# A two-block layer kernel: panel z behind panel k2, and the scan's exponential and norm moved in the written order

## The reference

```python
h = rmsnorm_2(x, norm_mix_w[l]) * (1 + sc_m) + sh_m
z, xbc, dt_raw, q, k, v = jnp.split(h @ w_in[l], IN_SPLITS_2, axis=-1)
y_ssd = ssd_mixer(z, xbc, dt_raw, ...)      # ends: rmsnorm_2(y * silu(z), norm_w)
y_att = chunk_attention(q, k, v, rel_bias[l])
x = x + g_m * (jnp.concatenate([y_ssd, y_att], axis=-1) @ w_out[l])
```

## Time and profile before

| | |
|---|---|
| median of 3 runs | 820.22 us (819.9 to 821.61) |
| the profiled execution | 820.22 us, span 818.5 us |
| TensorE busy | 797.6 us, 97% of the span |
| VectorE busy | 588.6 us, 72% |
| ScalarE busy | 496.8 us, 61% |
| GpSimd busy | 15.7 us, 2% |
| mean granted TensorE clock | 0.999 of full |
| HBM | 196 GB/s over the span |

### The profile page before, as it was taken

How to read it: one execution, slowest core, us unless ns; L and a number is a source line. 1 busy time by engine, 2 the same in 40 slices (tenths; PEclk the granted TensorE clock), 3 DMA queues, 4 the chain that set the end, 5 groups by cost and what they waited for, 6 DMA issues and landing times.

```text
span 818.5 us, 14145 instructions
## 1 busy us (share of the span) xinstructions
PE 797.6 (97%) x5904; PEld 742.7 (91%) x5904; DVE 588.6 (72%) x752; ACT 496.8 (61%) x745; POOL 15.7 (2%) x36
## 2 busy tenths in 40 slices
PE   8999999999999999999999999999999999999996
PEld 8988879999999879999998888899788999999885
DVE  5465776648766857887878896897776977787563
ACT  6778688558837456444344256856757776666452
POOL 3000000100200000000000000000000000000000
PEclk9999999999999999999999999999999999999999
DMA  8873534446452568889787992744251865646611
GB/s 277 303 230 133 191 119 154 156 154 218 165 185 104 160 199 266 270 294 300 254 299 277 340 355 94 238 153 152 98 164 53 281 191 170 193 145 205 226 57 52
DMA packets 105951, 161.13 MB, mean 197 GB/s; under 512 B 4496, under 2 KB 51872, under 8 KB 105888
## 3 DMA queue, kind: packets, MB, share of 16 engines
q1 hardware_dynamic: 105888, 160.24, 59.3%
HBM read 159.16 MB, written 1.06 MB: 196 GB/s over the span
## 4 chain that ended last, share of the span: by engine, by line
PE 85%; DVE 6%; ACT 5%; issue 2%; DMA 1%; SPq 0%; DVEq 0%; ACTq 0%
PE ps L1557 54%; PE ps L1560 22%; DVE wL L1031 2%; ACT wH L669 2%; PE ps L1491 2%; DVE arena L1031 2%; PE ps L1708 1%; ACT arena L916 1%; PE ps L1537 1%; DMA raw<-in_w_in 1%; PE ps L1675 1%; DVE arena L1034 1%; PE ps L1755 1%; PE ps L1752 1%; DVE res L1031 1%
## 5 line engine op out<-in xcount | busy, mean ns | idle before, releaser
L1031 DVE TENSOR_TENSOR wL<-raw,wH 128x2048 fp32r<-128x2048 f32 (+2 forms) x133 | 282.9, 2131 | 121.0 <-ACT wH L669 119.8
L1557 PE MATMUL ps<-p1H,wH 128*128 128x256 f32 x1256 | 359.0, 286 | 5.7 <-DVE p1L L1031 1.8
L1557 PE MATMUL ps<-p1L,wH 128*128 128x256 f32 x1256 | 355.3, 283 | 0.0
L1557 PE MATMUL ps<-p1H,wL 128*128 128x256 f32 x1256 | 355.3, 283 | 0.0
L669 ACT ACTIVATE wH<-raw 128x2048 fp32r<-128x2048 f32 (+1 forms) x121 | 225.1, 1867 | 123.2 <-PE ps L1557 65.3
L1557 PEld LDWEIGHTS ps<-p1H,wH 128*128 128x128 f32 x1256 | 240.8, 192 | 9.1 <-issue 6.7
L1557 PEld LDWEIGHTS ps<-p1L,wH 128*128 128x128 f32 x1256 | 240.9, 192 | 0.3 <-issue 0.2
L1557 PEld LDWEIGHTS ps<-p1H,wL 128*128 128x128 f32 x1256 | 240.8, 192 | 0.0
L1560 PE MATMUL ps<-wH,zH 128*128 128x512 f32 x176 | 68.6, 390 | 0.0
L1560 PE MATMUL ps<-wH,zL 128*128 128x512 f32 x176 | 68.5, 389 | 0.0
L1560 PE MATMUL ps<-wL,zH 128*128 128x512 f32 x176 | 68.5, 389 | 0.0
(11 more groups left out here) (248 smaller groups left out, 933.6 us busy)
## 6 DMA issues: line engine op xcount, KB each, us to landing
raw<-in_w_in SPq DMA_DIRECT2D x38, 1024.0 KB, 5.1
raw<-in_w_ada SPq DMA_DIRECT2D x24, 1024.0 KB, 5.2
raw<-in_w_up SPq DMA_DIRECT2D x44, 512.0 KB, 4.7
raw<-in_w_ffn_gate SPq DMA_DIRECT2D x22, 512.0 KB, 4.6
raw<-in_w_ffn_up SPq DMA_DIRECT2D x22, 512.0 KB, 5.7
raw<-in_w_ffn_down SPq DMA_DIRECT2D x10, 1024.0 KB, 5.6
raw<-in_w_down SPq DMA_DIRECT2D x10, 1024.0 KB, 5.2
raw<-in_w_out SPq DMA_DIRECT2D x8, 1024.0 KB, 5.1
```

The lines of the kernel that those rows point to most:

```text
L1031: return v.tensor_tensor(o, a, b, op)
L1557: last = mm(ps[:, t[1], 0:T], wt[:, slot, k, t[2]:t[2] + P], at_[:, k0 + k, :], start=st, stop=en)
```

## The change

In the list, product k2 is put where z was, and z where k2 was. With z go the waits of its neighbours: sY 0 and sC 1 now stand behind k2's first panel, sY 1 and the bias mask behind its second with the start of unit 6; unit 7's scores stand behind z's first panel; the transposes of unit 6, yz and unit 8's scores behind its second; the transposes of unit 7 and ysum behind v2's first panel, snorm and the transposes of unit 8 behind its second. The rounding and subtraction at z's two places (for the panels two places on) are put into X(7) and X(8), and those at v2's places are done at the panel. ACT's exponential over SG moves from the entry sC to the entry sA of the same group. The scratch places of SG's and CB's second halves and the PSUM bank of ysum move, since k2 is now written while SG's second half is in use, and bank 7 is used by transposes ahead of ysum. The transposes of unit 6 wait for sY's last evacuation in place of ysum's.

```diff
--- before.py
+++ after.py
@@ -96,7 +96,7 @@
 GATE_OF = {1: 0, 3: 1}
 
 LATER = {("out1", 1): 1, ("down1", 5): 2, ("oo1", 1): 3}
-BESIDE = [("ga0", 0), ("ga1", 0), ("hq0", 0), ("hf0", 0), ("hi0", 0), ("hg0", 0), ("k2", 1), ("v2", 0), ("v2", 1)]
+BESIDE = [("ga0", 0), ("ga1", 0), ("hq0", 0), ("hf0", 0), ("hi0", 0), ("hg0", 0), ("k2", 1), ("z", 0), ("z", 1)]
 NORM_OF = {"q0": 0, "f0": 1, "xs": 2, "u0": 3}
 RES = {1: "out", 2: "down", 3: "oo", 4: "dd"}
 
@@ -172,10 +172,10 @@
     gemm("xs", [("h_final",)])
     gemm("bc", [("dt_turn",)])
     gemm("q2", [("sA", 0)], [("sC", 0), ("sA", 1)])
-    gemm("z", [("sY", 0), ("sC", 1)], [("sY", 1), ("yz",)])
-    gemm("k2", [("ysum",), ("bias",), ("snorm",)], X(6, "k2", 1))
-    gemm("v2", X(7, "v2", 0) + [("pt", 6)], X(8, "v2", 1) + [("pt", 7)])
-    gemm("oo0", [("pv", 6), ("pv", 7), ("pt", 8)], only=0)
+    gemm("k2", [("sY", 0), ("sC", 1)], [("sY", 1), ("bias",)] + X(6, "k2", 1))
+    gemm("z", X(7, "z", 0), [("pt", 6), ("yz",)] + X(8, "z", 1))
+    gemm("v2", [("pt", 7), ("ysum",)], [("snorm",), ("pt", 8)])
+    gemm("oo0", [("pv", 6), ("pv", 7)], only=0)
     gemm("oo1", [("pv", 8)], only=0)
     gemm("oo0", only=1)
     gemm("oo1", [], [("norm", 3)], only=1)
@@ -423,7 +423,7 @@
         hV, hG = scr(58, TB, 512), scr(62, 4, T)
         YF = scr(66, 4, T), T1
         XC, XR = scr(0, 8, T), scr(8, 4, T + 3)
-        SG, CB, XD = (scr(22, 4, 384), scr(52, 4, 384)), (scr(28, 384), scr(58, 384)), scr(30, TB, 512)
+        SG, CB, XD = (scr(22, 4, 384), scr(38, 4, 384)), (scr(28, 384), scr(44, 384)), scr(30, TB, 512)
         sY, sZ, sT = scr(34, 4, T), scr(38, 4, T), scr(42, 4, T)
         q2, k2, v2, relb = scr(46, 4, T), scr(50, 4, T), scr(58, TB, 512), scr(62, 8, T)
         TG, ZT = scr(60, 2, T), scr(62, 2, T)
@@ -460,7 +460,7 @@
         ext_dram = nc.dram_tensor("ext_dram", (8, 384), F32).ap()
 
         ps = ctx.enter_context(nc.psum_tensor("ps", [P, 8, 512], F32))
-        ysum, rb = ps[:, 7, 0:T], ps[:, 7, T:2 * T]
+        ysum, rb = ps[:, 0, 0:T], ps[:, 7, T:2 * T]
         rbs = scr(69, T)
 
         def adaps(where, x):
@@ -993,7 +993,7 @@
                     nc.scalar.activation(DE[:], DA[:], ACT.Exp).then_inc(on.dt_e, 1)
                     act.wait_ge(on.dt_e, 1)
                     nc.scalar.activation(DE[:], DE[:], ACT.Ln, bias=1.0).then_inc(on.dt_ln, 1)
-                elif k == "sC":
+                elif k == "sA":
                     table(ACT.Exp)
                     act.wait_ge(on.seg, e[1] + 1)
                     nc.scalar.activation(SG[e[1]], SG[e[1]], ACT.Exp).then_inc(on.seg_exp, 1)
@@ -1683,7 +1683,7 @@
                         pe.wait_ge(on.yT_done, min(u, NU1))
                         pe.wait_ge(on.pt_done, u)
                     if u == NU1:
-                        pe.wait_ge(on.yln, 1)
+                        pe.wait_ge(on.sy, 4)
                         pe.wait_ge(on.cb, 2)
                     for b in range(8):
                         last = tr(pt67[:, b * P:(b + 1) * P], PR[u][:, b, :])
```

## The result

The changed kernel takes 830.93 us (median of 4 runs, 829.95 to 831.85) against 820.59 us in 4 runs of the kernel before (819.9 to 821.61). The ratio is 1.0125, with a 95% interval of 1.0105 to 1.0144: it is slower. The forecast was 827.8 us with a range of 825.5 to 831.5; rival 1, in which the clock falls as well, had 830.6 us. The profiled execution took 830.78 us with a span of 829.0 us, so the span grew by 10.5 us.

A forecast was written before the change was run, and what follows sets the result against it. TensorE's fixed order of work bounds the kernel, so only its idle time could change: stalls of 0.4 + 3.6 + 5.2 less 1.4 us won gave +7.8, the other way +7.5; taken +7.6 on 820.2, 827.8 us, range 825.5 to 831.5.

The forecast's parts named there:

- rival 1: The clock falls to half in the stall before oo0's first panel: +2.8 us, 830.6 us; chance 0.24.
- the stretch: The reordered part of TensorE's timeline, 545 to about 602 us; idle there was to total at least 5 us.
- the course that I held likeliest: Steps 1 to 5 with the clock full: +7.6 us, 827.8 us; chance 0.58.
- Step 1: ACT's exponential of SG0 ahead of a weight split delays q2's evacuation: TensorE stalls 0.4 us.
- Step 2: ACT's exponential of SG1 ahead of z's rounding makes G1 late: TensorE stalls 3.6 us before sY1.
- Step 3: Attention units 6 to 8: nothing stalls, and the old idle of 0.68 and 0.73 us is won.
- the two old spots: TensorE's old idle before unit 6's scores (0.68 us) and before unit 6's transposes (0.73 us), expected to go.
- Step 4: ACT's queue is full from 577 to 597 us, with a 1.29 us table load back to Exp before unit 8.
- my chain: The forecast's walk through ACT's and DVE's queues in the new order, with no pause for ACT from 577 to 597.
- Step 5: snorm stands behind oo1's subtraction on DVE, so TensorE stalls 5.2 us before oo0's first panel.
- The rule on Ln and Exp: One table load serves both functions in ysum; by it step 4 ends 1.3 us earlier and the time is 826.5 us.
- The one hold of 4.7 us or more: At the old trace's end TensorE kept full clock while idle, 812.0 to 816.7 us; a 3.6 us stall seemed safe.

The follow-up runs named there:

- the filled kernel: Changed kernel with 14 unread identity matmuls in the stall ahead of sY1 and 19 ahead of oo0's first panel: 828.16 us.
- The filled kernels: Unread identity matmuls in the long stalls: changed kernel with 14 and 19, 828.16 us; old order with the exponential in sA and 14, 823.61 us.
- the first filled kernel: Changed kernel with 30 unread identity matmuls ahead of sY1 and 42 ahead of oo0's first panel, which overran the stalls: 835.46 us.
- snorm ahead of the split: Changed kernel with the weight split at v2's second panel put behind snorm: 824.88 us.
- exponential undone: Changed kernel with ACT's exponential over SG back in the entry sC: 825.49 us.
- Silu left out: Changed kernel with z evacuated by Copy and not by Silu, so two table loads go: 828.22 us.

## Why the prediction was right, and where it was short

The direction, the two stalls and their makers were as forecast; TensorE's waits in the stretch are 8.5 us together (0.21, 3.47 and 4.80), above the 5 us under which the prediction called itself wrong. The measured time lies in the range, but it is rival 1's time and not the course that I held likeliest.

- **Step 1** (0.4 us at k2's first panel): the changed kernel's waits show 0.7 us in two places, of which 0.5 stand before q2's first panel as in the old trace. k2's first panel starts at 546.61, 0.63 later than in the old trace, and 0.2 of that is the stretch as a whole (the exponential of SG0 starts at 542.9 for 542.7): so 0.4 us.
- **Step 2** (3.6 us before sY1): 3.47 us in the trace, with DVE idle for 3.35 us before the subtraction at 558.13 (forecast 557.95). Shown to be the exponential's place by taking it out of the new order (the stall goes) and by putting it alone into the old one (the stall comes).
- **Step 3** (the two old spots go, nothing stalls here): they went. One new wait was overlooked: with the clock full, TensorE waits 0.34 us for ACT's evacuation of z before v2's first panel (the filled kernel, 582.09). In the changed kernel the fall of the clock hides it.
- **Step 4** (ACT full from 577, a fifth load in the stretch): of the five loads one stands at 537.91, with the exponential that moved forward, and four behind 577. ACT waited only once between 577 and 599, 2.2 us for DVE's maximum of unit 7, which my chain has at the same place. The load back to Exp before unit 8 is there (585.31). I took the upper bound for it and that was right. The two loads without the Silu were worth 2.1 us of stall.
- **Step 5** (5.2 us before oo0, snorm behind the split): 4.80 us, and 5.16 us with the clock full, filling included. Moving the split alone took 3.7 us of the 4.80.
- **The rule on Ln and Exp.** The Trainium skill (ScalarE: Activation LUTs, "Table sets: the hidden batching unit") has them share a set. The changed kernel's trace again has a load for each, at 593.36 and 595.24, so the page's rule does not hold here.
- **The clock** is the step that was short. I gave it 0.24, one stall, and a price of 2.8 us, and held that the stall of 3.6 us was below what the clock had outlasted at the kernel's end. In fact it fell twice, once behind each stall. The first fall slowed TensorE by 1.6 us (0.77 in sY1, 0.8 in the scores), of which 0.9 reached the end, and the second cost 1.4 us. The filled kernels show 2.1 to 2.8 us for both and 1.5 to 2.4 us for one alone. That rival 1's figure of 830.6 is so near 830.9 is in part luck: near the right total, but with one fall instead of two. The one hold of 4.7 us or more at the end of the old trace was a single sample, and I read it as a bound. At the ends of the ten traces the clock fell between 2.3 and 5.3 us after TensorE's last matmul; the 5.0 us of the old trace are near the longest. The Trainium skill (TensorE: Matmul & The Clock Gate, "Why this matters for your kernels") warns of such gaps between bursts; here the trace agrees with the page: the clock fell behind stalls of 3.5, 4.8 and 5.0 us, and it did not fall behind those of 2.7 and 1.1 us. These are single executions and give no bound: in the first filled kernel it fell behind a wait of 1.35 us, too, which it outlasts in the other nine traces.

The sum of the traces: 8.0 us for the queues with the clock full (7.5 to 7.8 in the prediction), 0.9 + 1.4 us for the clock, and 0.2 us that the stretch began later, 10.5 us in all.

## What to carry to other kernels

On an engine that goes through its list in order, moving a step forward moves everything behind it back, up to the moment when the step's own input is ready; look first at what the engine's other readers want from behind it, here the weight rounding. Put the steps that feed the bound engine next ahead of those that are only early. And when a stall of a few microseconds on TensorE is forecast, price the lower clock behind it too, from any such stall in a trace and not from one long hold. What the engine loses at the lower clock is an upper bound of that price, as later waits can take part of it in.

## What the runs showed of the hardware beyond that

- In the changed kernel the clock fell 0.6 us after TensorE had started again behind the stall of 3.5 us (564.16), and matmuls ran at half level with TensorE busy all the time until 568.2. So the stall itself can look innocent in the clock's row, which is 1.00 from 560.5 to 564.1. The moment varies: behind the same stall it fell 1.2 us after the restart with the old order (fall at 565.6, restart at 564.34), and 0.2 us before it with snorm ahead of the split (fall at 563.1, restart at 563.26).
- The stay at half level lasted 3.4 us in five of the seven falls in mid-kernel, and 6.8 us in two (exponential undone, Silu left out). In the six behind the long stalls it slowed TensorE by 1.4 to 2.8 us.
- An identity matmul in plain float32 with 128 columns is two records in the profile and takes 0.227 us, as long as one record of 512 columns in the rounded format (0.227 us from start to start on line 1560).
- Matmuls whose results nobody reads kept the clock full in the long stalls and gave back 2.1 to 2.8 us in the changed kernel and 1.5 to 2.4 us in the old order. They don't pay as such here, as kernels without the stalls are faster still (820.2 us).
